# 896 columns of an expert table as a dense product with picks taken out by one-hots, and decay sums spread through outside memory

## The reference, cut to what matters

```python
def _peer(xn, wq, k1, k2, U, V):
    q = (xn @ wq).reshape(B, L, PH, PEER_DK)                 # PH = 8 heads
    s1 = einsum('blhd,hnd->blhn', q[..., :half], k1)          # 128 first keys
    s2 = einsum('blhd,hnd->blhn', q[..., half:], k2)          # 128 second keys
    v1, i1 = top_k(s1, 16);  v2, i2 = top_k(s2, 16)
    # the 16 best of the 256 sums; expert = i1 * 128 + i2
    gate = softmax(top_s)
    h = gelu(einsum('thkd,td->thk', U[idx], x))               # table one
    return einsum('thk,thkd->td', gate * h, V[idx])           # table two
```

## Time and profile before

| | us |
|---|---|
| median of 3 runs | 3890.54 (3885.16 to 3890.75) |
| profiled run, its own time | 3897.42 |
| its span in the profile | 3895.7 |
| PE busy | 3328.9 (85%) |
| DVE busy | 1768.7 (45%) |
| ACT busy | 706.2 (18%) |
| POOL busy | 980.8 (25%) |
| read from outside memory | 793.08 MB |

### The profile page before, as it was taken

How to read it: one execution, slowest core, us unless ns; L and a number is a source line. 1 busy time by engine, 2 the same in 40 slices (tenths; PEclk the granted TensorE clock), 3 DMA queues, 4 the chain that set the end, 5 groups by cost and what they waited for, 6 DMA issues and landing times. The chain is left out here.

```text
span 3895.7 us, 38072 instructions
## 1 busy us (share of the span) xinstructions
PE 3328.9 (85%) x15208; PEld 2677.5 (69%) x15208; DVE 1768.7 (45%) x2953; ACT 706.2 (18%) x1537; POOL 980.8 (25%) x705
## 2 busy tenths in 40 slices
PE   8999999999999975002236999999999999999999
PEld 6878887888888865001114555555888888889888
DVE  5883011100000789998888444445245344444200
ACT  0002112100002110007678000002121122222100
POOL 0001000000000147876775555454000111112000
PEclk9999998999999987555557999999999999999999
DMA  5333432344544799999994999996333222222342
GB/s 215 141 130 143 147 110 76 130 152 154 198 188 151 315 389 368 375 356 351 377 377 154 331 333 338 346 337 241 135 116 133 90 87 76 87 76 76 138 154 97
DMA packets 118679, 797.65 MB, mean 205 GB/s; under 512 B 15064, under 2 KB 15704, under 8 KB 49640
## 3 DMA queue, kind: packets, MB, share of 16 engines
q1 hardware_dynamic: 61160, 426.10, 30.0%
q0 software_dynamic: 57344, 369.13, 25.0%
HBM read 793.08 MB, written 2.10 MB: 204 GB/s over the span
## 5 line engine op out<-in xcount | busy, mean ns | idle before, releaser
L355 PE MATMUL PS<-mem,ring 128*128 128x256 f32 (+1 forms) x4608 | 1033.8, 387 | 3.0 <-DMA ring<-in_first_tiles 3.0
L355 PEld LDWEIGHTS PS<-mem,ring 128*128 128x128 f32 x4608 | 881.8, 192 | 152.9 <-issue 4.7
L972 POOL DMA_INDIRECT mem<-in_peer_u,idx x256 | 522.8, 2042 | 1169.6 <-DVE idx L1423 908.9
L1775 PE MATMUL PS<-mem,ring 128*128 128x256 f32 x2816 | 642.5, 383 | 9.9 <-DVE ring L2161 9.9
L1458 DVE CUSTOM_DVE_ANT_0 mem<-mem 128x2048 f32<-128x2048 f32 x256 | 585.4, 2287 | 80.1 <-DMA mem<-in_peer_u,idx 79.1
L1775 PEld LDWEIGHTS PS<-mem,ring 128*128 128x128 f32 x2816 | 530.5, 192 | 84.5 <-issue 16.3
L1524 DVE SCALAR_TENSOR_TENSOR mem<-mem 128x768 f32<-128x768 f32 x256 | 261.0, 1019 | 284.9 <-DMA mem<-in_peer_vg,idx 278.5
L1139 PE MATMUL PS<-mem 128*128 128x128 f32 x512 | 140.4, 398 | 263.1 <-ACT mem L1253 252.1
L990 POOL DMA_INDIRECT mem<-in_peer_vg,idx x256 | 284.6, 1112 | 265.4 <-DVE mem L1524 225.6
L1139 PEld LDWEIGHTS PS<-mem 128*128 128x128 f32 x512 | 98.4, 254 | 305.4 <-ACT mem L1253 209.6
L1751 POOL TENSOR_TENSOR mem<-mem,ring 128x512 f32<-128x512 f32 x84 | 113.1, 1365 | 774.7 <-DVE mem L2269 566.6
(11 more groups left out here) (342 smaller groups left out, 2939.6 us busy)
## 6 DMA issues: line engine op xcount, KB each, us to landing
ring<-in_first_tiles SPq DMA_DIRECT2D x144, 1024.0 KB, 4.8
ring<-in_dn_tiles SPq DMA_DIRECT2D x88, 1024.0 KB, 4.8
mem<-in_peer_vd SPq DMA_DIRECT2D x128, 640.0 KB
ring<-in_out_panels SPq DMA_DIRECT2D x16, 2048.0 KB, 7.8
ring<-in_w_out SPq DMA_DIRECT2D x8, 2048.0 KB, 8.9
ring<-in_peer_wq SPq DMA_DIRECT2D x8, 2048.0 KB, 8.9
ring<-in_mem_w_kv SPq DMA_DIRECT2D x8, 2048.0 KB, 11.5
mem<-in_x SPq DMA_DIRECT2D x4, 1024.0 KB, 7.1
```

What stands on the lines that cost most here:

```text
L355: last = nc.tensor.matmul(PS[:, 4 + n % 4, 0:T if wide else TX], wslot[:, slot_of[n], k, :], x, start=(k == 0), stop=(k == KT - 1))
L972: nc.gpsimd.indirect_dma_start(Ug[:, at % US, :], None, a["peer_u"][0], bass.IndirectOffsetOnAxis(ap=idx[:, n, j:j + 1], axis=0)).then_inc ...
L1775: ins = nc.tensor.matmul(bank_of(n), wts[:, n % WS, k, :], hT[:, k, :], start=(k == 0), stop=(k == KT - 1))
```

## The change

Table one is split like table two. Its columns 0 to 895 (`CU = 896`) are multiplied as a dense product with all tokens' `xn` (turned): 128 blocks, one for each first key, of seven products of 128 experts x 256 tokens, accumulated in PSUM, from buffers `Ut` that SP fills (459 KB a block). ACT takes each block out into the same matrices `weights_of` that the scatter uses later. Columns 896 to 2047 are still gathered (0.59 MB a gather) and multiplied by DVE.

A token's 128 picks are then taken out of its sums in two steps. The second keys of all tokens go to outside memory (`pick_dram`) and come back spread over all partitions, four tokens a group (`oh`); POOL compares them with the partition index, which makes one-hots; PE multiplies the one-hots with the token's 128 x 128 sums (`pick_products`); DVE keeps the first key's entry and sums (`pick_sums`). A transpose brings the result back to rows of tokens, `whole_dots` scales it and adds the gathered part, gelu runs once for 128 tokens, and softmax weights are applied once per half.

The order: dense product after the memory's keys and values on PE; the picks of the first half beside the gathers of `n = 12`; the picks of the second half spread over the 44 steps after that. The scatter gives ACT only the first 64 tokens and DVE, ACT and POOL together the other 192. All searches but the first two lie in the first seven rounds of gathers. Keys and values of the memory are taken out at once and wait in outside memory (`kx_dram`, `vx_dram`); so does the residual (`h_dram`), whose place in `h_tok` the normed tokens and two `Ut` buffers take.

In stage two the running sums are written to outside memory once (`decay_dram`), and each group's rows come back spread over all partitions on ACT's queue, one group ahead. `gsel` and the two products L1861 go. Level 0 uses PE's transpose.

```diff
-                    for i in range(2):
-                        load_turn(sp, wq_panel, i, G_WQ)
+                    load_turn(sp, wq_panel, 0, G_WQ)
+                    sp.wait_ge(h_added, 4 * RING)
+                    sp.dma_start(h_dram, h_tok).then_inc(h_spilled, 16)
+                    load_turn(sp, wq_panel, 1, G_WQ)
...
+                    for i in range(NKEY):
...
+                        if i == UT:
+                            sp.wait_ge(kk_taken, TPI)
+                            sp.dma_start(kx_dram, kx_s).then_inc(kv_spilled, 16)
+                            sp.wait_ge(kv_taken, TPI)
+                            sp.dma_start(vx_dram, vx_s).then_inc(kv_spilled, 16)
+                        if i >= UT:
+                            sp.wait_ge(u_done, i - UT + 1)
+                        sp.dma_start(Ut[i % UT], a["peer_ud"][i]).then_inc(ut_in[i % UT], 16)
+                        if i == 104:
+                            sp.wait_ge(found, HN)
+                            sp.dma_start(pick_dram.rearrange("m t k -> t m k"), keys[:, :, 1, :]).then_inc(keys_spilled, 16)
+
+                    for g in range(MT * NPG):
+                        if g >= PG:
+                            sp.wait_ge(pk_done, g - PG + 1)
+                        sp.dma_start(oh[:, g % PG, :, :],
+                                     pick_dram[g // NPG, 4 * (g % NPG):4 * (g % NPG) + 4, :].unsqueeze(0).broadcast_to([P, 4, P])
+                                     ).then_inc(oh_in[g % PG], 16)
...
                             nc.gpsimd.indirect_dma_start(
-                                Ug[:, at % US, :], None, a["peer_u"][0],
+                                Ug[:, at % US, :], None, a["peer_ug"],
                                 bass.IndirectOffsetOnAxis(ap=idx[:, n, j:j + 1], axis=0)).then_inc(u_in[at % US], 16)
+                            for g in pick_groups(at):
+                                pool.wait_ge(oh_in[g % PG], 16 * (g // PG + 1))
+                                x = oh[:, g % PG, :, :].rearrange("p q k -> p (q k)")
+                                nc.gpsimd.tensor_scalar(x, x, pidx, None, ALU.is_equal).then_inc(oh_made, 1)
...
+                    for i in range(NKEY):
+                        pe.wait_ge(ut_in[i % UT], 16 * (i // UT + 1))
...
+                        for k in range(KU):
+                            last = nc.tensor.matmul(PS[:, i % BANKS_U, 0:TX], Ut[i % UT][:, k * P:(k + 1) * P], xnD[:, k, :],
+                                                    start=(k == 0), stop=(k == KU - 1))
+                        last.then_inc(u_done, 1)
...
+                    def pick_products(g):
+                        m, t = divmod(4 * g, P)
+                        pe.wait_ge(oh_made, g + 1)
+                        if g < BANKS_U:
+                            pe.wait_ge(u_out, MT * NKEY)
+                        else:
+                            pe.wait_ge(picked, 4 * (g - BANKS_U + 1))
+                        for q in range(4):
+                            last = nc.tensor.matmul(PS[:, g % BANKS_U, q * P:(q + 1) * P], oh[:, g % PG, q, :],
+                                                    weights_of[m][:, :, t + q], start=True, stop=True)
+                        last.then_inc(pk_done, 1)
...
+                    for g in range(NPG):
+                        pick_products(g)
+                    picked_transpose(0)
+                    for g in range(AHEAD):
+                        pick_products(NPG + g)
+                    weight_transpose(0)
+                    for n in range(HOT0):
+                        scatter(n)
+                        if n % 4 == 3:
+                            for g in range((NPG - AHEAD) * (n // 4) * 4 // HOT0, (NPG - AHEAD) * (n // 4 + 1) * 4 // HOT0):
+                                pick_products(NPG + AHEAD + g)
+                    picked_transpose(1)
+                    for n in range(HOT0, MT * P):
...
+                    def pick_sums(g):
+                        m, t = divmod(4 * g, P)
+                        dve.wait_ge(pk_done, g + 1)
+                        for q in range(4):
+                            x = PS[:, g % BANKS_U, q * P:(q + 1) * P]
+                            nc.vector.scalar_tensor_tensor(x, iota[:, :], turnk[:, m, 0, t + q:t + q + 1], x, ALU.is_equal, ALU.mult,
+                                                           accum_out=hp[:, m, t + q:t + q + 1]).then_inc(picked, 1)
...
+                            if n == FIRST_PICK and j == 0:
+                                softmax_gates()
+                                dve.wait_ge(it_out, 1)
+                            for g in pick_groups(at):
+                                pick_sums(g)
...
-                        for m in range(MT):
-                            nc.tensor.matmul(PS[:, m, :], ones[0:VH, :], gsel[:, :, m * P:(m + 1) * P],
-                                             start=True, stop=True).then_inc(rows_done, 1)
...
+                                    if l == 0:
+                                        last = nc.tensor.transpose(to, No[:, m, h, :], ident[:, :])
+                                    else:
+                                        last = nc.tensor.matmul(to, No[:, m, h, :], Y[:, m, h, :], start=True, stop=True)
...
+                        act.dma_start(decay[:, i % 2, :, :], decay_dram[VG * i:VG * (i + 1), :].unsqueeze(0).broadcast_to([P, VG, TX])
+                                      ).then_inc(decay_in[i % 2], 16)
```

## The result

The changed kernel takes 3947.05 us (median of 4 runs, 3941.93 to 3954.51), the kernel before 3890.64 beside it: ratio 1.0147, 95% interval 1.0125 to 1.0169. It is 56 us slower, where +27 was forecast.

The account below looks back on a forecast made before the run. Gather DMA was taken to bound table one, PE table two's product and stage two. Later scatter end +50, table two +3 and decays -26 gave +27, 3917.5 us; range 3875 to 3985, the forecast's own 3898 to 3945.

Parts of the forecast that it names:

- the decays: Stage two: removed products, PE's wait in the first group and cheaper level 0 save 26 us.
- the way to the first scatter: Eight second-half pick groups ahead of the weight transpose, at 2.4 us a step: 22 us, ending at 1980.
- the tail: After the 64th scatter: the last pick group's sums, four gathers and the start of one-hots, 8 us, to 2110.
- the last tokens: 192 tokens scattered by DVE, ACT and POOL together: 83 us, last scatter at 2193.
- group 0: First group of stage two: PE's 5.20 us wait, 3.71 of products and 2.2 of slow records go, 11.1 us.
- PE's product takes the place of the DMA bound: Dense product of table one: 387 us on PE, ending at 1878, so the saved gather bytes are worth nothing.
- Rival 4: Dense product of table one not always fed, or the clock drops in it: plus 39 us, 3956; chance 0.10.
- The first round: Picks of the first 128 tokens, paced by POOL at 4.8 us a step: 80 us, bounds 57 and 110.
- Table two, plus 3: Table two stage: 1 MB of keys loaded in a DMA-busy stage adds 3 us for the last gather.
- Rival 2: Picks cost little and the decay saving outweighs the rest: 3884.5 us, or 3875.5; chance 0.17.
- Rival 3: The loop through outside memory paces the picks, 110 us for the first half's: plus 30, 3947; chance 0.20.
- The shared port: First half's picks: POOL comparisons and two-input DVE dot products exclude each other, making them up to 23 us longer.

Follow-up runs that it names:

- hot32: The whole change with ScalarE alone making one-hot rows for 32 tokens instead of 64, second half's weights turned at token 48: 3938.79 us, ratio 1.0126.
- tail_late: The whole change with the first four loads of table two's dense columns held back until the last gathered row is used: 3947.80 us, ratio 1.0139.
- experts_only: The whole change less its decay part, so the new expert layer with the decay sums of before: 3964.96 us, ratio 1.0198.
- pool_quarter: The whole change with GpSimd comparing only the first 128 of each 512 columns (picks not the reference's): 3926.08 us in one execution.
- ahead4: The whole change with 4 instead of 8 second-half pick groups ahead of the turn of the first half's weights: 3936.08 us, ratio 1.0107.
- decays_only: The kernel before with only the decay part of the change, its expert layer as before: 3874.52 us, ratio 0.9956.
- rows_not_columns: The whole change with pick products reading 128 neighbouring numbers instead of ones 512 bytes apart (picks not the reference's): 3954.29 us in one execution.

## Why the prediction was right or wrong

The order of the stretches, what stands in series and the sign came as forecast. The measured 3947 lies just above the forecast's own range (3898 to 3945). The sum failed by terms that were wrong in size: the decays, counted at 26 and worth 15.6 in this trace, the way to the first scatter, the tail, and the last tokens. The largest is the decays, and its failed step is group 0, where the removed wait and products were counted as gained in full.

**Right in place and sign.** PE's product takes the place of the DMA bound, bytes saved are worth nothing, and picks, ScalarE's tokens and the rest stand in series behind it. The keys and values end at 1491.8 (1488, of which 3.6 is the execution), the product takes 386.9 us (387), VectorE waits 63 us (55), ScalarE's 64 tokens take 122 us (122). Rival 4 is out: the stream was fed, at clock 1.00.

**The first round: right by two errors.** I took 4.8 us a step of POOL and 80 us; 81.3 were measured. But the comparison takes 1.88 us on average, not 1.2, and lies outside the bound of 1.365 that I had from a product of 128x512; a gather issue takes 1.07 us, not 2.06. Two comparisons and an issue are 2 x 1.88 + 1.07 + 0.18 = 5.0. The groups of POOL from 1879 to 1961:

```profile
L1051 POOL TENSOR_SCALAR mem<-mem 128x512 f32<-128x512 f32 x30 | 56.3, 1882 | 5.2 <-DMA mem<-second_keys 4.5
L1043 POOL DMA_INDIRECT mem<-in_peer_ug,idx x17 | 18.2, 1073 | 3.0 <-issue 3.0
```

The sums on VectorE follow each other at 0.27 us, at the lower bound and not at the 0.36 I took; as POOL paced the round, it didn't matter here. That 81.3 lies so near 80 is luck twice over: kernels with the same code take 75.9 to 83.2.

**The way to the first scatter: a wrong engine.** I gave eight groups VectorE's pace, 2.4 us a step, "POOL runs some three steps ahead". POOL was not ahead; it had just paced the round before. In those 28 us it makes 7 comparisons (13.6 us) and 11 issues (13.1). This is a term of the sum that was mis-sized, 22 for 28 (30 to 32 in hot32, tail_late and experts_only, where it is the same code), and pool_quarter (21) and ahead4 (11.5) show the cause.

**The tail and the 192 tokens: 8 for 16, 83 for 87.** What I left out is a transfer of the change itself: SP sends 2.6 MB of table two as soon as the last pick product is done, and the last gather lands behind them (4.40 us of waiting, above); VectorE had also come late to the gather's release, since it waited 5.46 us for PE. tail_late takes the 4.40 away, and VectorE's first one-hot comes 4 us sooner. Then POOL issues four gathers of table two before its first comparison, for which PE waits 2.91 us. PE's timeline of the kernel after:

```profile
2126.94 1.62 PE L1232 MATMUL PS<-mem 128*128 128x128 f32 x6 [10.57 <-DVE mem L1590]
2131.47 1.83 PE L1232 MATMUL PS<-mem 128*128 128x128 f32 x7 [2.91 <-POOL mem L1063]
```

**Table two, plus 3: right number, wrong cause.** The stage is 2.5 us longer in the change. But decays_only, which carries nothing of memory's keys through this stage, has PE waiting 9.5 us at its end, and experts_only, which does, 6.8, as before (6.7). So it is not the keys; how the last gathered rows land would do it, which no run shows.

**Decays, minus 26 for 15 to 17: the step that failed is group 0.** I counted the stall of 5.20 us, the 3.71 of the products and the slow 2.2 as gained without asking what comes late next. ScalarE's copies did, done at 3053.1 where VectorE was done at 3050.7, and the removed products had been their cover. A wait of 4.34 us stands where 5.20 stood, the records behind it run at the low clock as before, and 5.2 us are gained of 11.1: six of the nine us that decays_only lacks in its trace (17.1 for 26). Most of the rest is in the later groups, of which one gains 0.9 where 2.8 were forecast.

So of the 30 us by which the sum was short, 10 are the decays, 6 the way to the first scatter, 8 the tail, 4 the last tokens and about 4 the execution, less 2 for a quicker hand-over to the first pick (on the medians the miss is 29). Rival 2 fell with the size of the comparison. Rival 3 named 3947, the time measured, by coincidence: its round of 110 us took 81, in which POOL waits 4.5 us for the loop, and once GpSimd is relieved the round is 67 to 69 us, with PE the busiest engine.

**The shared port.** In the timeline of the change the length of two comparisons of POOL depends on whether a dot product of VectorE lies beside them. POOL's timeline of the kernel after:

```profile
1910.27 3.13 POOL L1051 TENSOR_SCALAR mem<-mem 128x512 f32<-128x512 f32 x2
1913.57 1.03 POOL L1043 DMA_INDIRECT mem<-in_peer_ug,idx  x1 [0.17 <-issue]
1914.62 4.21 POOL L1051 TENSOR_SCALAR mem<-mem 128x512 f32<-128x512 f32 x2
...
1920.06 4.19 POOL L1051 TENSOR_SCALAR mem<-mem 128x512 f32<-128x512 f32 x2
```

VectorE's dot products in the same stretch of it:

```profile
1907.97 1.36 DVE L1603 CUSTOM_DVE_ANT_0 mem<-mem 128x1152 f32<-128x1152 f32 x1 [0.55 <-DMA mem<-in_peer_ug,idx]
1914.37 1.47 DVE L1603 CUSTOM_DVE_ANT_0 mem<-mem 128x1152 f32<-128x1152 f32 x1 [2.57 <-DMA mem<-in_peer_ug,idx]
1919.69 1.56 DVE L1603 CUSTOM_DVE_ANT_0 mem<-mem 128x1152 f32<-128x1152 f32 x1 [1.64 <-DMA mem<-in_peer_ug,idx]
```

A pair alone takes 3.13 us. The pair from 1914.62 has a dot product beside it until 1915.84, 1.22 us, and takes 1.08 more; that from 1920.06 until 1921.25, 1.19 us, and takes 1.06 more. POOL gets next to nothing done while a dot product that started first runs. The other way round VectorE waits: POOL's comparison from 1984.96 takes its 1.58 us, and the dot product that starts 0.13 us into it takes 1.79 in place of 1.36. Over the 32 comparisons of the round that is 32 x (1.88 - 1.57) = 10 us, not the 23 that I gave as the upper end, as many of them fall beside sums from PSUM or started first. This agrees with the Trainium skill, "SBUF — State Buffer", on the shared port pair: exclusive, and held for a whole instruction.

## What to carry to other kernels

When a change turns one long bound into several short stretches in series, size each stretch by every engine that works in it, GpSimd's DMA issues included; the engine that paced the last stretch is not ahead in the next. Before a removed instruction is counted as gained, look for the chain that ended under it. When columns move from a gather to a dense product, find the split at which both end together: of the two splits tried here, 896 columns with rebalanced engines were still slower than the kernel before, and 768 brought the expert layer level with it. And before a gain is put down to the main part of a change, set the whole against the run with the small part alone. When two paces of an instruction are compared, compare them at the same granted clock.

## What the runs showed of the hardware

GpSimd compares 128x512 numbers with a number per partition in 1.57 us alone, more than its product of two tensors of that size costs on average (1.365); a column costs 2.5 ns (shortest 1.553 for 512 columns, 0.602 for 128 in pool_quarter). Its gather issue takes 0.93 us at the shortest in both kernels, for rows of 2048 and of 1152 numbers, 1.07 on average where VectorE mostly works from PSUM, and 2.06 where a dot product on two inputs of SBUF is nearly always under way. A sum from PSUM with accumulator read steps at 0.27 us although its parts are listed at 0.35 and 0.14: they overlap. A pick product reads its moving operand 512 bytes apart at 0.226 us a record and neighbouring numbers at 0.12, both at the full granted clock (rows_not_columns); at half the clock both take 0.22 to 0.24.
